# One extra unread product at thirteen places in TensorE's stream of a two-layer hybrid encoder

## The reference

```python
def token_mix(xn, past, w_in, b_f, w_branch, w_gate, w_out):
    (a_q, a_k, a_v, i_q, i_k, i_w, b_q, b_k, b_v, c_q, c_k, c_v, c_f) = jnp.split(xn @ w_in, points, axis=-1)
    ...
    o_a = sweep_queries(lambda qp, q, qi, wi: dsa_block(...), pos, a_q, i_q, i_w)      # top-k sparse attention
    o_b = sweep_queries(lambda qp, q: sb_block(...), pos, b_q)                        # stick-breaking
    o_c = sweep_queries(lambda qp, q, f: fox_block(...), pos, c_q, fq)                # forgetting attention
    o = jnp.stack([o_a, o_b, o_c], axis=2).reshape(B, T, N_BRANCH, BRANCH_W)
    branch = jnp.einsum('btnw,nwd->btnd', o, w_branch)
    gate = jax.nn.sigmoid((xn @ w_gate).reshape(B, T, N_BRANCH, D_MODEL))
    return jnp.einsum('btnd,btnd->btd', gate, branch) @ w_out, new_rows

def conv_ffn(xn, conv_past, w_up, conv_w, conv_b, w_down):
    h = xn @ w_up
    ...                                                                              # causal width-3 depthwise conv
    return (jax.nn.silu(g) * u) @ w_down, hp[:, -(CONV_W - 1):]

for l in range(DEPTH):
    m, rows = token_mix(rmsnorm(x, norm_mix[l]), ...)
    x = x + m
    f, conv_state = conv_ffn(rmsnorm(x, norm_ffn[l]), ...)
    x = x + f
```

## Time and profile before

| | |
|---|---|
| median of three runs | 2098.59 us |
| the profiled execution's own time | 2098.73 us |
| its span | 2096.9 us |
| TensorE matmul busy | 2079.0 us (99%) |
| TensorE weight loads busy | 1973.1 us (94%) |
| VectorE busy | 1393.5 us (66%) |
| ScalarE busy | 1004.0 us (48%) |
| GpSimd busy | 228.7 us (11%) |
| mean granted TensorE clock | 0.999 of full |
| DMA | 83 GB/s |

### The profile page before, as it was taken

How to read it: one execution, slowest core, us unless ns; L and a number is a source line. 1 busy time by engine, 2 the same in 40 slices (tenths; PEclk the granted TensorE clock), 3 DMA queues, 4 the chain that set the end, 5 groups by cost and what they waited for, 6 DMA issues and landing times.

```text
span 2096.9 us, 39540 instructions
## 1 busy us (share of the span) xinstructions
PE 2079.0 (99%) x15814; PEld 1973.1 (94%) x15822; DVE 1393.5 (66%) x2612; ACT 1004.0 (48%) x1635; POOL 228.7 (11%) x162
## 2 busy tenths in 40 slices
PE   8999999999999999999999999999999999999998
PEld 8888988898999999999998989889989999999998
DVE  7658657878747763676465786588787377636753
ACT  6267315646626652444352772255565366424432
POOL 0023000000031110011310220000001301001112
PEclk9999999999999999999999999999999999999999
DMA  6231222121222223222232212221212222222222
GB/s 204 77 106 41 91 81 98 54 77 51 61 81 81 82 88 91 90 80 91 91 108 81 94 43 91 82 95 53 79 51 63 79 90 80 91 91 81 89 84 94
DMA packets 53763, 175.03 MB, mean 83 GB/s; under 512 B 6720, under 2 KB 11408, under 8 KB 53632
## 3 DMA queue, kind: packets, MB, share of 16 engines
q1 hardware_dynamic: 47168, 158.88, 24.5%
q0 software_dynamic: 2688, 9.95, 1.2%
q10 hardware_dynamic: 3776, 4.34, 0.7%
HBM read 160.25 MB, written 12.90 MB: 83 GB/s over the span
## 4 chain that ended last, share of the span: by engine, by line
PE 97%; DVE 2%; ACT 1%; issue 0%; DMA 0%; DVEq 0%; SPq 0%; ACTq 0%
PE d L1499 63%; PE d L1547 14%; PE ab L1593 4%; PE d L1880 2%; PE d L1558 2%; PE d L1889 2%; PE ab L1819 1%; PE ab L1831 1%; PE d L1597 1%; PE ab L1868 1%; PE ab L1499 1%; PE ab L1813 0%; PE ab L1645 0%; PE d L1736 0%; PE ab L1676 0%
## 5 line engine op out<-in xcount | busy, mean ns | idle before, releaser
L481 ACT ACTIVATE wh<-raw 128x512 fp32r<-128x512 f32 x548 | 345.1, 631 | 718.1 <-PE d L1499 564.7
L853 DVE TENSOR_TENSOR wl<-raw,wh 128x512 fp32r<-128x512 f32 x548 | 387.7, 710 | 284.7 <-ACT wh L481 275.9
L1499 PE MATMUL d<-xh,wh 128*128 128x288 f32 x2400 | 513.2, 295 | 6.8 <-DVE wl L851 6.8
L1499 PE MATMUL d<-xl,wh 128*128 128x288 f32 x2400 | 510.8, 294 | 0.0
L1499 PE MATMUL d<-xh,wl 128*128 128x288 f32 x2400 | 510.7, 293 | 0.0
L1499 PEld LDWEIGHTS d<-xh,wh 128*128 128x128 f32 x2400 | 383.2, 188 | 11.3 <-issue 10.1
L1499 PEld LDWEIGHTS d<-xl,wh 128*128 128x128 f32 x2400 | 383.1, 188 | 0.0
L1499 PEld LDWEIGHTS d<-xh,wl 128*128 128x128 f32 x2400 | 383.0, 188 | 0.0
L1547 PE MATMUL d<-xh,wh 128*128 128x288 f32 x768 | 173.5, 307 | 0.0
L1547 PE MATMUL d<-xh,wl 128*128 128x288 f32 x768 | 164.6, 295 | 0.0
L1547 PE MATMUL d<-xl,wh 128*128 128x288 f32 x768 | 164.2, 295 | 0.0
(11 more groups left out here) (321 smaller groups left out, 3260.8 us busy)
## 6 DMA issues: line engine op xcount, KB each, us to landing
raw<-in_w SPq DMA_DIRECT2D x286, 512.0 KB, 3.5
out_o_k<-k POOLq DMA_DIRECT2D x4, 1152.0 KB, 7.7
out_o_v<-v POOLq DMA_DIRECT2D x4, 1024.0 KB, 8.8
x<-in_xT SPq DMA_DIRECT2D x8, 288.0 KB, 5.4
k<-in_bc_k_past ACTq DMA_DIRECT2D x4, 512.0 KB, 4.4
v<-in_bc_v_past ACTq DMA_DIRECT2D x4, 512.0 KB, 6.6
out_y<-z SPq DMA_DIRECT2D x4, 432.0 KB, 2.7
raw<-in_w SPq DMA_DIRECT2D x4, 256.0 KB, 5.8
```

The costliest lines, as they stand in the source:

```text
L481: act.activation(wh[:, c % SPLIT_SLOTS, :], stored, ACT.Copy).then_inc(high_done, 1)
L853: dve.tensor_tensor(lows, stored, highs, ALU.subtract).then_inc(low_done, 1)
L1499: ins = pe.matmul(outs[half], w_, r_[:, kk, HALF * half:HALF * half + HALF], start=first and n == 0 and begin, stop=last and n == len(kks) ...
```

## The change

A helper `odd_product` issues one product: the first 128 x 128 high weight block of the chunk that the following projection starts with, against the first 128 columns of the activations, written to columns 800 to 928 of the bank (512 + 288 on), which nothing reads. It is called in the branch outputs of every mixer (`branch_first`), in `project(l, U_SMALL, D_SMALL)` of layer 1, in `project(l, U_K[B] + 2, ...)`, in `project(l, U_Q[A] + 3, ...)`, and in `up(f, 0, 1)` behind the norm sum. In all that is thirteen products.

```diff
--- before.py
+++ after.py
@@ -1521,8 +1521,16 @@
                     wait_low(pe, l, r, kk)
                 return wait
 
-            def project(l, u, d, wait=no_wait):
+            def odd_product(before, d, c, src):
+
+                pe.wait_ge(low_done, before + c + 1)
+                pe.matmul(dbank[d % 2][:, 512 + HALF:512 + HALF + P], wh[:, c % SPLIT_SLOTS, 0:P],
+                          src[:, 0, 0:P], start=True, stop=True, skip_group_check=True)
+
+            def project(l, u, d, wait=no_wait, odd=False):
                 pe.wait_ge(dfree[d % 2], freed(l, d))
+                if odd:
+                    odd_product(l * CHUNKS, d, 2 * u, xh)
                 dense(l * CHUNKS, wait, 2 * u, dhalf[d % 2], xh, xl, range(KD))
 
             def project_half(l, u, d, b):
@@ -1571,6 +1579,8 @@
 
                 pe.wait_ge(dfree[d % 2], freed(l, d))
                 pe.wait_ge(low_done, l * CHUNKS + c + 1)
+                pe.wait_ge(oh_ready, l * 12 + 4 * m + 1)
+                odd_product(l * CHUNKS, d, c, oh)
                 for kk in range(4):
                     pe.wait_ge(oh_ready, l * 12 + 4 * m + kk + 1)
                     high_products(0, kk)
@@ -1615,7 +1625,7 @@
                     dense(l * CHUNKS, no_wait, 2 * (U_IQ + 1), iq1_out, xh, xl, range(KD))
                 wait_taken(pe, l, D_KI)
                 pe.sem_inc(dfree[D_PASSED % 2], 1)
-                project(l, U_SMALL, D_SMALL)
+                project(l, U_SMALL, D_SMALL, odd=l > 0)
                 project_half(l, U_Q[B], D_Q[B], 0)
 
                 wait_taken(pe, l, D_SMALL)
@@ -1763,7 +1773,7 @@
                         pe.wait_ge(v_taken, l * 8 + 4)
                         pe.wait_ge(sample_apart, l + 1)
                         logits_z(0)
-                        project(l, U_K[B] + 2, D_K[B] + 2)
+                        project(l, U_K[B] + 2, D_K[B] + 2, odd=True)
                         project(l, U_K[B] + 3, D_K[B] + 3)
 
                         for p in range(PAIRS):
@@ -1918,7 +1928,7 @@
                             pe.wait_ge(chosen_ready, l + 1)
                             scores_wide(0)
                             scores_next(0)
-                            project(l, U_Q[A] + 3, D_Q[A] + 3)
+                            project(l, U_Q[A] + 3, D_Q[A] + 3, odd=True)
                             gate_blocks(l, m, 0, range(0, 4))
                         for p in range(PAIRS):
                             t4 = base4 + 4 * p
@@ -1974,15 +1984,17 @@
                 for j in range(KD):
                     project(l, U_OUT + j, D_OUT + j, xn_wait(l, 1) if j == 0 else no_wait)
 
-                def up(f, i, s, wait=no_wait):
+                def up(f, i, s, wait=no_wait, odd=False):
                     pe.wait_ge(dfree[s], START + l * (D_USES // 2) + f * (D_HALF // 2) + i + D_UP // 2)
+                    if odd:
+                        odd_product(l * CHUNKS, s, 2 * U_UP + 2 * s, xh)
                     dense(l * CHUNKS + f * (2 * U_HALF) + 4 * i, wait, 2 * U_UP + 2 * s, dhalf[s], xh, xl, range(KD))
 
                 for f in range(2):
                     if f == 0:
                         up(f, 0, 0, xn_wait(l, 2))
                         norm_sum(2 + 2 * l)
-                        up(f, 0, 1)
+                        up(f, 0, 1, odd=True)
                     with pe.Fori(1 - f, FH) as i:
                         for s in range(2):
                             up(f, i, s)
```

## The result

The changed kernel takes 2121.31 us (median of 5 runs, 2121.26 to 2122.73) against 2098.59 us: a ratio of 1.0108, 95% interval 1.0097 to 1.0120. It is slower by 22.7 us. The forecast was 2089.6 and its range ended at 2111; the time lies above it, 0.7 us from the sum of the first rival (2120.6).

A forecast was written before the change was run, and what follows sets the result against it. TensorE was taken as the bound, by product count times pitch. A gain of 10.4 us less 1.4 us cost gave 9.0 net: 2098.6 - 9.0 = 2089.6 us, range 2087.5 to 2111.

The forecast's parts named there:

- the first rival: Feed-forward parts of both layers go slow behind the added product: 20.6 us, 2120.6 with nothing gained elsewhere; chance 0.25.
- What bounds the kernel: TensorE, busy 2079.0 of 2096.9 us: product count times pitch, 130.0 or 133.3 ns; VectorE and ScalarE have room.
- The cost: Thirteen added products at 0.11 us each, taken from 128-column rows: 1.4 us, between 0.7 and 2.5.
- The gain: Slow stretches behind the new products turn fast: 3144 products at 3.3 ns, 10.4 us.
- if one product turns slow into fast: Condition for gaining 10.4 us in the slow stretches; the trace had no product inserted alone to show it.
- two-way alternation: Hidden inside TensorE, in or out of step with the pairs; one product more shifts later pairs by one place.
- That the product behind the norm sum keeps the feed-forward part at 130.0: Ahead of `up(f, 0, 1)`: restores the fast pitch after the norm sum; no new gain, costs 0.11 us.
- The feed-forward part turns slow: Product behind the norm sum throws its fast stream back: 20.6 us; 2120.6, or 2110.2 with branch gains kept; chance 0.25.
- The gain is given back further on: Value products behind branch B turn fast into slow; 216 products lose 0.7 us per layer: 2091.0; partial gains together 0.20.
- Nothing turns over: Kind of work sets the state, so a lone product changes nothing: only 1.4 us cost, 2100.0 us; chance 0.12.

The follow-up runs named there:

- probes: Unread products of several kinds and widths put into the long streams of the kernel before, at 45 places; 2131.77 us (one run).
- the placed kernel: Kernel before plus six products: 48 products into C's and A's branch outputs, and one ahead of each first up projection; 2094.77 us, ratio 0.9979.
- the 4 placed two later: Six added products in the kernel before, the four in C's and A's branch outputs at 50 products instead of 48; 2099.88 us, ratio 1.0002.

## Why the prediction was wrong

**What bounds the kernel** held: TensorE's pitch, its two values, and no waits. The expectation that VectorE and ScalarE have room held as well.

**The cost** held in number: 13 x 0.11 = 1.4 us. That was luck, since its row was misread. The three products of the earlier trace rows that take 0.113 us each are passes of plain float32, two to a product, not the streams' own type, and the high end of 0.19 us is not a pass of the norm sum, which takes 0.24. The added product starts 0.05 to 0.06 us ahead of the next (590.21 to 590.27), and the rest of the 0.11 us lies in the pair behind it.

**The gain** is the step that failed: "if one product turns slow into fast". I took the state for a two-way alternation that any single product turns over. It is a cycle of four, and of the two places between pairs a product leads out from one only. In the change, ten of the eleven products that were to earn something stand right behind value products, logits or scores, ahead of the stream and not in it, where there is no settled cycle yet; the eleventh (the small projection's) met a stream that the norm sum had made fast. None of them brought anything: the stretches behind the branch outputs read 133 ns, and 3144 products at 3.3 ns, 10.4 us, came to nothing.

**That the product behind the norm sum keeps the feed-forward part at 130.0,** because a norm sum turns fast into slow, failed twice. With mixer A's products in, the norm sum meets a slow stream, but one behind, and leaves it slow; and had it left it fast, the product behind would have undone that, as the run with those two alone shows. Either cause by itself makes both feed-forward parts slow (2120.65 and 2119.65 us).

**The rivals.** "The feed-forward part turns slow" was right in place and price (20.6 + 1.4 on top of 2098.6), though it counted 3168 and 3054 products behind the added ones where 3216 and 3105 stand, and the range left the price of both layers out, though the rival had 0.25. Its mechanism was half of it: I had the product behind the norm sum do the damage to a stream that the norm sum makes fast as before; the shift of the cycle by a product 624 products earlier was not in it. "The gain is given back further on" named C's key projections, and they are slow after, 1.4 us; but there was no gain to give back, and they are slow in kernels without a product ahead of B's branch output as well. By the traces, the value products leave a fast stream when they come one behind and a slow one when they come three behind. "Nothing turns over" had the right objection: the transposes of layer 0 and 1 do not fit a switch by count. It had 0.12 and deserved more.

The evidence against was in the trace before. Every norm sum that met a slow stream there met it three behind; none came one behind, so that all of them agreed said nothing about that place. A look at the single gaps, instead of the means of windows, would have shown the cycle of four, and with it that the effect of one product could depend on its place.

## What to carry to other kernels

Where TensorE is full and equal products run at two pitches, look at the single starts, not at the mean, and find what repeats and after how many products. A product put into such a stream moves the place in the cycle of what comes later, up to a stretch many microseconds on, so the first thing to check after any edit on a full TensorE is the pitch of the longest stretch. Here some 3.3 ns for each of 6321 products made 20.6 us, fifteen times what the thirteen products themselves cost.

## What the runs showed of the hardware

- Streams of 288-column pairs in rounded float32 at the full clock (2.4 GHz level, granted 1.00) run at 130.0 or at 133.3 ns a product, and stay there for more than 3000 products across loops, bank changes and semaphore waits, until something else comes.
- One rounded product of 64 to 224 columns that comes three behind the 140 ns gap makes a slow stream fast, in 10 of 10 cases (5 probes, the 4 of the placed kernel's branches, the small projection's). One that comes one behind never did, in 10 of 10 (3 probes, the 4 placed two later and the 2 ahead of the first up projections in that kernel, and the small projection's where only the two behind the norm sums were taken out). One of 32 to 128 columns in a fast stream made it slow in 6 of 6; a plain float32 product of 288 columns left it fast in 8 of 8. What inside TensorE runs through four steps is not shown by any run.
- The state at the start varies between profiles of kernels that are alike up to there: the stretch behind the first norm sum is fast in five (before among them) and slow in four (after among them). In the five the norm sum comes three behind, in the four one behind. The granted clock rises within the first 24 products, mostly at another one in each trace, but three traces in which it rises at the same one (the 20th) end in two fast stretches and a slow one, so that alone doesn't set it; what does is open. It is 108 products, 0.4 us.
- A product started anew in a bank whose other columns hold an open sum changed the outputs (relative error 0.062, in the kernel with the four products two later; with all six outside open sums the outputs stayed right). That the first pair's part is what is lost is not shown.
